# Routing stage of a hybrid decoder layer: experts sorted ahead of the gates, first expert loads asked for at the table, first up product ahead of the last shared steps

## What is computed

```python
def moe(h, w_router, b_router, we_g, we_u, we_d, ws_g, ws_u, ws_d):
    s = jax.nn.sigmoid(jnp.dot(h, w_router))
    sb = s + b_router                        # 8 groups of 8 experts
    gscore = sum of the 2 best sb in each group;  4 best groups stay
    eidx = top_k(sb of those groups, 8)      # 8 of 64 experts for each token
    wts = s[eidx] / sum(s[eidx]) * 2.5       # the gates
    # for each expert e and its tokens:
    #   acc[tok] += wt * ((silu(h[tok] @ we_g[e]) * (h[tok] @ we_u[e])) @ we_d[e])
    shared = (silu(h @ ws_g) * (h @ ws_u)) @ ws_d
    return routed + shared
```

## Time and profile before

| what | value |
|---|---|
| median of 3 runs | 1111.59 us |
| profiled execution, its own time | 1111.61 us |
| its span, first to last instruction | 1109.8 us |
| mean granted TensorE clock in it | 0.994 of full |
| PE busy | 1068.0 us, 96% |
| DVE busy | 698.6 us, 63% |
| ACT busy | 218.0 us, 20% |
| POOL busy | 135.4 us, 12% |
| DMA moved | 337.14 MB, mean 304 GB/s |

### The profile page before, as it was taken

One profiled execution on the slowest core, in us unless ns is written; L12 is line 12 of the kernel. 1 busy time (PEld: TensorE's weight loads), 2 busy tenths in 40 slices (PEclk: granted clock), 3 DMA queues, 4 the chain that ended last, 5 costly groups with the idle time before them and its releaser, 6 DMA issues.

```text
span 1109.8 us, 16863 instructions
## 1 busy us (share of the span) xinstructions
PE 1068.0 (96%) x6139; PEld 542.4 (49%) x6139; DVE 698.6 (63%) x1857; ACT 218.0 (20%) x478; POOL 135.4 (12%) x163
## 2 busy tenths in 40 slices
PE   6999999999999999999999999989999999899886
PEld 3456678777877644664343433333343333233232
DVE  3218441556545644862369888869888889688157
ACT  4131332322233213301111111101111111111111
POOL 0110000000020020111111121211111111111100
PEclk9999999999999999999999999989999999999999
DMA  9858721020262277869999999999999999999698
GB/s 368 337 203 305 232 80 45 32 86 4 112 197 80 76 243 248 313 220 421 404 425 424 424 425 422 425 423 410 414 426 422 425 424 423 422 420 387 243 419 341
DMA packets 51655, 337.14 MB, mean 304 GB/s; under 512 B 9637, under 2 KB 14089, under 8 KB 30831
## 3 DMA queue, kind: packets, MB, share of 16 engines
q1 hardware_dynamic: 33710, 287.32, 63.9%
q0 software_dynamic: 17856, 48.68, 11.6%
HBM read 311.30 MB, written 37.24 MB: 314 GB/s over the span
## 4 chain that ended last, share of the span: by engine, by line
PE 88%; DMA 7%; DVE 2%; issue 1%; ACT 1%; SPq 0%; DVEq 0%; POOLq 0%; ACTq 0%
PE bank L1565 29%; PE bank L1588 15%; PE bank L1260 10%; PE bank L1279 5%; DMA mem<-expert_out_rows 3%; PE bank L1378 3%; DMA mem<-in_w_exp_down 3%; PE bank L1379 3%; PE bank L1496 3%; PE bank L1173 3%; PE bank L1257 3%; PE bank L1148 1%; PE bank L1576 1%; PE bank L1131 1%; PE bank L1343 1%
## 5 line engine op out<-in xcount | busy, mean ns | idle before, releaser
L1565 PE MATMUL bank<-mem 128*32 128x512 f32 (+2 forms) x1504 | 330.3, 606 | 11.0 <-issue 10.4
L1565 PEld LDWEIGHTS bank<-mem 128*32 128x32 f32 (+2 forms) x1504 | 106.1, 129 | 191.8 <-issue 191.8
L2261 DVE STREAM_TRANSPOSE mem<-mem 32x256 f32<-32x256 f32 x400 | 174.2, 436 | 5.2
L1588 PE MATMUL bank<-mem 128*32 128x512 f32 (+2 forms) x752 | 164.4, 596 | 1.1 <-ACT mem L1069 1.1
L1260 PE MATMUL bank<-hT,mem 128*128 128x288 f32 x512 | 133.3, 409 | 1.0 <-ACT mem L939 1.0
L1565 PE MATMUL bank<-x_sb,mem 128*32 128x512 f32 (+2 forms) x400 | 111.2, 603 | 0.0
L1260 PEld LDWEIGHTS bank<-hT,mem 128*128 128x128 f32 x512 | 93.8, 190 | 25.8 <-issue 2.4
L2261 DVE STREAM_TRANSPOSE mem<-x_sb 32x256 f32<-32x256 f32 x208 | 90.6, 436 | 2.7
L1588 PEld LDWEIGHTS bank<-mem 128*32 128x32 f32 (+2 forms) x752 | 52.1, 127 | 72.1 <-issue 71.4
L2277 DVE COPY hT<-bank 128x512 f32<-128x512 f32 x48 | 33.2, 691 | 60.0 <-PE bank L1588 59.9
L1069 ACT ACTIVATE mem<-bank 128x256 f32<-128x256 f32 x48 | 18.4, 384 | 263.4 <-PE bank L1576 263.2
(11 more groups left out here) (404 smaller groups left out, 1258.1 us busy)
## 6 DMA issues: line engine op xcount, KB each, us to landing
mem<-k_w_exp SPq DMA_DIRECT2D x52, 2048.0 KB, 22.1
mem<-in_w_exp_down SPq DMA_DIRECT2D x52, 1024.0 KB, 23.8
x_sb<-k_w_exp SPq DMA_DIRECT2D x12, 2048.0 KB, 24.8
mem<-k_w_ada SPq DMA_DIRECT2D x8, 2048.0 KB, 9.3
mem<-k_w_in SPq DMA_DIRECT2D x7, 2048.0 KB, 8.9
hT<-in_w_exp_down SPq DMA_DIRECT2D x12, 1024.0 KB, 25.9
mem<-expert_out_rows SPq DMA_DIRECT2D x6, 2048.0 KB, 17.0
mem<-k_w_head SPq DMA_DIRECT2D x4, 2048.0 KB, 18.8
```

The source lines that it names most:

```text
L1565: i = mm(bank[sl, :], xT[:, j % 2, c * BLK + sl.start:c * BLK + sl.stop], wview(r)[0][:, c, :], start=c == 0, stop=c == KC - 1)
L1588: i = mm(ps[4 + hf][sl, :], hhT[:, k * BLK + sl.start:k * BLK + sl.stop], wview(r)[1][:, k, hf * 512:(hf + 1) * 512], start=k == 0, stop=k ...
L2261: i = dve.transpose(cols[dl, :, sl], rows[sl, :, dl])
```

## The change

It moves instructions in the stage between the mask and block 1, and swaps what lies where in slot 3.

- DVE: the sort, with the count copy (was L2146), comes first behind the mask, then the positions, a comparison for block 0 alone (`first_tokens`), the sorted ids, the token index of block 0 alone (`token_out`, signal `tok_ready`), then two shared multiplications, the gates, the rest.
- PE: a small product `find_tokens` (2 columns) gives block 0's token index; the full `find_idx(0)`, for gate and slot indices, comes later. The table's product comes 6 steps behind `positions`. `x_T(0)`, `find_idx(0)`, `find_idx(1)` and `up(0)` come ahead of the last 5 shared steps and `find_idx(2)`.
- POOL: gather 0 waits for `tok_ready`; the `bcG` loads come ahead of the gathers, behind the last `h2T` transposes. The counter `pool_step` is replaced by `over`.
- Slot 3 (`LATESLOT`) now has its down weights first and gate/up behind; the shared weights lie where the gate/up goes. At the table SP issues slot 4's gate/up and slot 3's down; at the last shared step slot 3's gate/up and slot 4's down.

```diff
@@ 305 @@
-        gu_s, e_ = carve(mem, v_at, [2, KC, FE])
+        gu_s, e_ = carve(mem, w2_at + FJ * D, [2, KC, FE])
         wr, e_ = carve(mem, e_, [KC, NE])
-        wsh = mem[:, v_at:e_]
+        wsh = mem[:, w2_at + FJ * D:e_]
@@ 468, wview @@
+            if slot(r) == LATESLOT:
+                gu = mem[:, at_ + FJ * D:at_ + WSZ].rearrange("p (c n) -> p c n", c=KC)
+                return gu, mem[:, at_:at_ + FJ * D].rearrange("p (j d) -> p j d", j=FJ)
@@ 634, SP @@
-            load_gate_up(NPRE, id3)
             load_gate_up(XSLOT, id4)
+            load_dn(LATESLOT, id3)
             sp.wait_ge(S["gu_mm"], NSH)
-            load_dn(NPRE, id3)
+            load_gate_up(LATESLOT, id3)
             load_dn(XSLOT, id4)
@@ 783, POOL @@
             pool.wait_ge(S["h2T_t"], NT)
+            pool.wait_ge(S["ld_bc"], 3 * SPREAD + 16)
+            spread(pool, bcG, 5, S["ld_bc"])
...
             def ahead(n, q, g):
-                pool.wait_ge(S["idx_ready"], n + 1)
+                if isinstance(n, int) and n == 0:
+                    pool.wait_ge(S["tok_ready"], 1)
+                else:
+                    pool.wait_ge(S["idx_ready"], n + 1)
@@ 1525, PE @@
             positions()
-            shared_up(12)
+            shared_up(6)
+            def find_tokens():
+                pe.wait_ge(S["P_ready"], 1)
+                pe.wait_ge(S["pos_done"], 1)
+                pe.wait_ge(S["gu_silu"], 2)
+                for tt in range(NT):
+                    i = mm(ps[6][:, 0:2], Pm[:, 0, tt, :], Re[:, 0, tt, 0, 0:2], start=tt == 0, stop=tt == NT - 1)
+                i.then_inc(S["pos_mm"], 1)
...
+            pe.wait_ge(S["srt_ready"], 1)
+            pe.wait_ge(S["gu_silu"], 1)
+            mm(ps[0][:, 0:2 * NE], ones[0:NE, :], sperm[0:NE].rearrange("p a e -> p (a e)"),
+               start=True, stop=True).then_inc(S["srt_mm"], 1)
+            shared_up(3)
+            find_tokens()
+            shared_up(12)
+            x_T(0)
             find_idx(0, 0, pieces(0))
-            shared_up(4)
             find_idx(1, 1, pieces(1))
-            shared_up(KC // 2)
...
-            shared_up(KC // 2)
-            x_T(0)
-            shared_up(2)
+            new_gu(0)
+            up(0, 0, pieces(0))
+            shared_up(5)
             find_idx(2, 2, pieces(2))
@@ 2226, DVE @@
+            def first_tokens():
+                cp(Re[:, 0, :, 0, 0:2], Rk[:, :, 0:4:3, 0])
+                stt(Pm[:, 0], pos[:, :, 0:1].to_broadcast([P, NT, P]), 0.0, iota.unsqueeze(1).to_broadcast([P, NT, P]),
+                    ALU.add, ALU.is_equal).then_inc(S["P_ready"], 1)
+            def token_out():
+                dve.wait_ge(S["pos_mm"], 2)
+                o = ps[6]
+                ts(idxg[:, 0:1], o[:, 0:1], o[:, 1:2], float(OOB), ALU.add, ALU.add).then_inc(S["tok_ready"], 1)
@@ 2283, DVE @@
-            place(0)
-            place(1)
-            idx_out(0, 0)
+            sort_keys()
+            places()
+            first_tokens()
+            sorted_ids()
+            token_out()
             for i in range(2):
                 shared_mul(i)
-            sort_keys()
-            idx_out(1, 1)
+            gates()
             shared_mul(2)
-            sorted_ids()
-            place(2)
+            cp(Re[:, 0, :, 0, :], Rk[:, :, :, 0])
+            place(1)
             xT_evac(0, 0)
+            idx_out(0, 0)
+            idx_out(1, 1)
+            place(2)
             shared_mul(NSH - 1)
             idx_out(2, 2)
```

More of the change, by code:

```diff
@@ L47 @@
 EXTSLOT = 0
+LATESLOT = 3
 XSLOT = 4
@@ L802, in ahead @@
                     pool.wait_ge(S["xT_ready"], n - XG + 1)
-                pool.sem_inc(S["pool_step"], 1)
+                pool.sem_inc(S["over"], 1)
                 gather(q, g)
@@ L1527, in _ @@
             positions()
-            shared_up(12)
-            def find_idx(n, j, parts):
-                pe.wait_ge(S["P_ready"], n + 1)
-                if not (isinstance(n, int) and n == 0):
+            shared_up(6)
[6 more added lines that the diff above has]
+                i.then_inc(S["pos_mm"], 1)
+            def find_idx(n, j, parts):
+                if isinstance(n, int) and n == 0:
+                    pe.wait_ge(S["P_ready"], 2)
+                    pe.wait_ge(S["tok_ready"], 1)
+                else:
+                    pe.wait_ge(S["P_ready"], n + 1)
                     pe.wait_ge(S["idx_ready"], n)
-                else:
-                    pe.wait_ge(S["pos_done"], 1)
-                    pe.wait_ge(S["gu_silu"], 2)
                 for tt in range(NT):
@@ L1624, in _ @@
             for b in range(NBK):
-                new_gu(b)
                 split = KC if b + 1 < TURNED else KC - 2
-                up(b, b, pieces(b), range(split))
+                if b >= 1:
+                    new_gu(b)
+                    up(b, b, pieces(b), range(split))
                 if b == 0:
@@ L2128, in _ @@
             dve.wait_ge(S["msk_ready"], 1)
[L2130 to L2134, removed]
             for t in range(NT):
@@ L2136, in _, with places @@
                 dve.tensor_tensor_scan(cumv[:, t, :], ones[:, 0:NE], maskm[:, t, :], 0.0, ALU.mult, ALU.add)
[L2137 to L2142, removed]
+            def places():
+                dve.wait_ge(S["pos_mm"], 1)
+                step(stt(pos, PV[:, 0:NT, :], FAR, maskm[:, 0:NT, :], ALU.add, ALU.mult))
+                ts(pos, pos, -FAR, None, ALU.add).then_inc(S["pos_done"], 1)
+                dve.wait_ge(S["pos_done"], 1)
@@ new lines, in gates @@
+            def gates():
+                step(tt_(sbias, smat, maskm[:, 0:NT, :], ALU.mult))
+                dve.tensor_reduce(stat[:, 12, 0:NCH], sbias[:, 0:NCH, :], AX.X, ALU.add)
+                step(dve.tensor_reduce(stat[0:NS, 12, NCH:NT], sbias[0:NS, NCH, :], AX.X, ALU.add))
+                step(dve.reciprocal(stat[:, 13, :], stat[:, 12, :]))
+                step(stt(sbias, sbias, ROUTED, stat[:, 13, :].unsqueeze(2).to_broadcast([P, NT, NE]), ALU.mult, ALU.mult))
+                step(cp(R[:, 1], sbias))
+                step(tt_(sbias, sbias, R[:, 1], ALU.subtract))
+                step(cp(R[:, 4], sbias))
+                tt_(R[:, 6], sbias, R[:, 4], ALU.subtract)
+                step(tt_(R[:, 5], R[:, 7], cumv, ALU.add))
@@ L2143, in _ @@
             PV = ps[4][:, 0:(NT + 1) * NE].rearrange("p (t e) -> p t e", t=NT + 1)
-            step(stt(pos, PV[:, 0:NT, :], FAR, maskm[:, 0:NT, :], ALU.add, ALU.mult))
-            step(ts(pos, pos, -FAR, None, ALU.add))
-            cp(ovf[:, 0, :], PV[:, NT, :]).then_inc(S["pos_done"], 1)
-            dve.wait_ge(S["pos_done"], 1)
             def sort_keys():
+                dve.wait_ge(S["pos_mm"], 1)
+                step(cp(ovf[:, 0, :], PV[:, NT, :]))
                 key, own, rank = cst["order"][:, 0, :], scol[0:NE, 0:1], scol[0:NE, 1:2]
@@ L2242, in idx_out @@
                 o = ps[6]
-                ts(idxg[:, q:q + 1], o[:, 0:1], o[:, 3:4], float(OOB), ALU.add, ALU.add)
+                if not (isinstance(n, int) and n == 0):
+                    ts(idxg[:, q:q + 1], o[:, 0:1], o[:, 3:4], float(OOB), ALU.add, ALU.add)
                 ts(wtab[:, q:q + 1], o[:, 1:2], o[:, 4:5], o[:, 6:7], ALU.add, ALU.add)
```

18 lines of the change are left out of this document (6 added, 12 removed).

## The result

The changed kernel took 1126.11 us (median of 4 runs, 1122.63 to 1126.67) against 1112.07 us for the kernel before on the same chip: ratio 1.0112, 95% interval 1.0098 to 1.0126, so **slower by 1.1%, 11 to 14 us**. The sign was forecast, the size was not: 1119.6 was named, and 1126.1 lies 1.6 us above the range. The profiled execution took 1126.52 us, its span is 1124.7 us, 14.9 more than before.

The account below looks back on a forecast made before the run. The load queue was taken to set the end, with PE counting only if late slot releases starve it. Block 3's release +9.3 us late, partly absorbed, gave +8.0: 1111.6 + 8.0 = 1119.6 us, range 1111.8 to 1124.5.

Parts of the forecast that it names:

- Part 2: Gather 0 beside early loads: lands in 8.3 us, PE idle 4.0 us before x_T(0), up(0) then loses 1.3 us of clock.
- Part 3: Last shared step to block 2: up(1) waits for DVE's block 3 comparison, starting +8.0 us; up(2) also waits 1.3 for gather 2.
- Part 4: Load queue: block 3's late release, less at most 2.5 us of queued work, makes later loads and the end +8.0 us.
- What bounds the kernel: Block loop: the end moves with the load queue; PE's lateness stays hidden unless late slot releases starve that queue.
- Part 1: Up to the first gather: gather 0 issued at 479.3 instead of 480.76, first loads at 479.3 to 479.8 instead of 485.5.
- Bounds here 0 and 3; I take 1.3: Half clock in up(0) after PE's idle time before x_T(0): 1.3 us lost, between 0 and 3.
- p = +9.3 us: Lateness of up(2), hence of block 3's slot release: 518.1 us against 508.77 before.
- less at most 2.5: Queue work left when block 3 frees its slots, near 528 us, absorbs at most 2.5 us of PE's lateness.
- The sign that I named for the middle: PE's weight waits in the middle of the loop would sum to less than 10.4 us.
- Rival 1: At x_T(0), gather 0 is not held up by the loads: 1112.6 to 1115.1 us, middle 1113.8; chance 0.18.
- Rival 2: Load queue starts 3 MB 6 us earlier and the loop keeps half: -3 us, 1108.6; chance 0.10.
- Rival 3: PE's lateness is absorbed by 10.4 us of weight waits and more queue stock at 528 us: 1111.6; chance 0.14.

Follow-up runs that it names:

- both parts undone: Changed kernel with up(0) back behind all shared steps and SP's table loads held until gather 0 has landed; 1116.37 us, ratio 1.0018.

## Why the prediction was right in kind and short in size

PE's lateness in the last block is 13.8 us in the trace, where +8.0 stood. Two steps make the difference: the clock, which carries most of the 4.6 us in Part 2 and Part 3, and the 1.3 us that Part 4 took off for a stock of work in the load queue.

- **What bounds the kernel:** right. Made late one at a time, the queue moved the end by 0.49% and PE, through its releases, by 0.77% (5.4 and 8.6 us of 1112). In the changed kernel the queue's own lateness was +9.1 us (rank 5's gate/up landed at 521.7, 15.7 us after its issue; +4.4 was named), still less than PE's, so the larger one won as forecast.
- **Part 1:** right within 0.6 us. SP's first load at 479.33 (479.3 named), gather 0 at 479.85 (479.3), PE before x_T(0) at 484.1 (483.6).
- **Part 2, gather 0:** the mechanism right, "I take 8.3 us" was 9.3. With the later issue x_T(0) stood at 489.17 instead of 487.6.
- **Part 2, the clock: the term that was mis-sized.** "Bounds here 0 and 3; I take 1.3" was 0.9 in the transposes and 2.2 in up(0), 3.1 together. In Part 3 I put nothing on the clock in up(1); it was 3.0. I had priced the clock by the idle time directly in front of a product; here a second, shorter idle time followed a long one, and this trace has a slow product behind each. This is the larger part of the miss: block 2 was 4.6 us later than I had it (13.9 for 9.3): +1.3 are gather 0, +0.9 the transposes behind it, +1.05 up(0) (9.35 for the 8.3 that held my loss), +1.7 the way from up(1) to up(2) (14.9 for 13.2: +3.0 of clock, -1.3 for the wait at x_T(2) that did not come, as PE was too late to see it), and -0.4 a shorter way from up(0)'s end to up(1). In all the clock cost 6.1 us in these products, where 1.3 were taken. The range closed at what the prediction gives for the upper ends together, +13 and 1124.6, and the 3.0 of up(1) were not among them.
- **Part 3, the comparison:** right. up(1) came 3.8 us behind the last shared step, 4.1 named; DVE L2232 is its releaser. Block 2: +14.1 where "p = +9.3 us" stood (from the positions +13.9).
- **Part 4, the step that was wrong in kind:** "less at most 2.5". I read a stock of work in the queue at 528 us from the 9.5 us of a 1 MB load, and took 1.3 us off. In every row of the table but that of the loads held back the lateness of up(3) arrives in the last block to 0.5 us: there is no stock. The sign that I named for the middle, weight waits of less than 10.4 us in all, did not come either (11.0). The row that I should have read is the rate of that stretch, 399 GB/s at 0.98 where the loop has 420 at 1.01.
- **Rival 1** (gather not held up) did not happen: gather 0 took 9.3 us. The run with the loads behind the gather comes near to what it would have cost: up(3) 2.9 us late, inside the rival's 2.7 to 4.2, and 1.0040, which is 4.5 us with an interval of 2.2 to 6.8, where the rival had 2.2 (1113.8). It was priced with the same reserve in the queue that Part 4 had wrong. By the Trainium skill (DMA: Bandwidth & Descriptors, "Anatomy of one DMA") a gather would take some 3.2 us, an estimate from that page; measured are 4.1 alone and 9.3 beside loads.
- **Rival 2** (faster) has nothing for it: no gain from the early loads showed even with gather 0 out of their way. **Rival 3** (absorbed) was refuted by the kernel with PE made late.

## What to carry over

Where engine and load queue run in a closed loop (a slot is released, its load is asked for), as here, the lateness of the tightest release went through to the end (9.1 us as 8.8, 13.9 as 13.8), and waits for weights later on were no reserve; look for it where the DMA rate first dips below that of the rest of the loop. Loads asked for earlier paid nothing here, since nothing waited for them, and they cost at once where a small transfer that an engine does wait for went out beside them (9.3 us for 4.3): issue that one first, or hold the loads until it has landed. A product moved ahead of filler work uncovers what the filler hid on the other engines: list those before moving.

## What I had not expected of the hardware

The granted clock fell in more places than the idle times suggested, and not in the same ones each time. In the changed kernel it was 0.50, 1.2 of 2.4 GHz, from 508 to 514 us, under up(1). With 5.06 us of waiting in front of x_T(0) PE went through x_T(0), a 1.09 us wait and the whole of up(0) at the lower level or partly so (0.50 granted from 493 to 497 us; 9.35 us for 7.11), and behind a wait of 2.07 us and one of 0.26 it fell again (10.09). The same 2.08 and 0.37 us gave 7.1 us in the run with the loads behind the gather, 8.80 with up(0) ahead alone and 8.63 with the token index first, and 1.81 and 0.62 us gave 8.80 with both parts undone; 1.46 us in front of x_T(2) gave no fall. I can name the cost of a fall (1.5 to 3.0 us on a 7.1 us product) and not which short wait will have one.
